# Hybrid mixer layer with grouped experts: weights in 8 KB runs, w2 by rows, combination one step later

## What is computed

```
h   = layer_norm(x) 
mix = hybrid_mixer(h)                # w_in (2048 x 5120), convolutions, gates, w_out (2048 x 2048)
h1  = layer_norm(alpha * h + mix)    # gain ln1_g, shift ln1_b
s   = sigmoid(h1 @ w_router)         # 32 experts in 8 groups of 4
# per token: the best group, and in it the best two experts; gates = s of the two, normalised
ffn = sum over the token's two experts e of gate * ((silu(h1 @ w1[e]) * (h1 @ w3[e])) @ w2[e])
out = layer_norm(alpha * h1 + ffn)   # gain ln2_g, shift ln2_b
```

## Time and profile before

| | |
|---|---|
| median of 3 runs | 1466.75 us (1466.39 to 1469.31) |
| profiled execution, span from first to last instruction | 1466.0 us |
| PE / DVE / ACT / POOL busy | 1296.9 / 455.2 / 353.1 / 243.0 us |
| moved by DMA | 473.81 MB, mean 323 GB/s |
| expert phase, from its first expert product | 419.2 us to about 1448 us |

### The profile page before, as it was taken

How to read it: one execution, slowest core, us unless ns; L and a number is a source line. 1 busy time by engine, 2 the same in 40 slices (tenths; PEclk the granted TensorE clock), 3 DMA queues, 4 the chain that set the end, 5 groups by cost and what they waited for, 6 DMA issues and landing times.

```text
span 1466.0 us, 17030 instructions
## 1 busy us (share of the span) xinstructions
PE 1296.9 (88%) x6870; PEld 721.7 (49%) x6870; DVE 455.2 (31%) x648; ACT 353.1 (24%) x530; POOL 243.0 (17%) x62
## 2 busy tenths in 40 slices
PE   3897989999989999998989898989989898998983
PEld 3887989978743433333433333333433333343331
DVE  5545995642352130311303031121303022130306
ACT  4332322443321121211212121121212121121211
POOL 3767586565100000000000000000000000000001
PEclk9998999999989999999999999999999999999997
DMA  7554535547789999999999999999999999999991
GB/s 275 165 173 144 173 127 189 173 172 251 253 311 387 387 387 387 387 387 387 387 387 387 387 387 387 387 387 387 387 387 387 387 387 387 387 387 387 387 387 76
DMA packets 237572, 473.81 MB, mean 323 GB/s; under 512 B 9594, under 2 KB 10170, under 8 KB 236642
## 3 DMA queue, kind: packets, MB, share of 16 engines
q1 hardware_dynamic: 234256, 471.90, 88.5%
q10 hardware_dynamic: 3282, 1.43, 0.5%
HBM read 471.20 MB, written 2.10 MB: 323 GB/s over the span
## 4 chain that ended last, share of the span: by engine, by line
PE 64%; DMA 13%; DVE 11%; SPq 5%; ACT 4%; issue 2%; POOL 1%; ACTq 0%; DVEq 0%
PE psum L629 16%; PE psum L603 15%; PE psum L643 8%; PE psum L576 8%; PE psum L452 8%; DMA ring<-in_w_dram 7%; PE psum L472 7%; DMA area_g<-in_w_dram 6%; SPq L308 5%; DVE area_g L988 4%; ACT area_c L842 2%; POOL w_low L392 1%; DVE area_a L1252 1%; DVE area_a L1066 1%; DVE area_a L1253 1%
## 5 line engine op out<-in xcount | busy, mean ns | idle before, releaser
L603 PE MATMUL psum<-ring,area_c 128*64 128x512 f32 x1536 | 340.4, 595 | 25.8 <-DMA ring<-in_w_dram 25.8
L392 POOL TENSOR_TENSOR w_low<-ring,w_high 128x2048 fp32r<-128x2048 f32 (+1 forms) x42 | 225.2, 5371 | 112.8 <-ACT w_high L707 112.8
L603 PEld LDWEIGHTS psum<-ring,area_c 128*64 128x64 f32 x1536 | 106.5, 137 | 240.2 <-issue 191.3
L842 ACT ACTIVATE area_c<-psum,ln_chan 128x128 f32<-128x128 f32 x264 | 99.2, 456 | 402.9 <-PE psum L576 402.9
L452 PE MATMUL psum<-in_high,w_high 128*128 128x256 f32 x576 | 168.2, 292 | 25.2 <-POOL w_low L392 9.3
L398 POOL TENSOR_TENSOR area_b<-area_b,area_c 128x1024 f32<-128x1024 f32 x1 | 3.2, 3234 | 1079.1 <-ACT area_b L878 1079.1
L629 PE MATMUL psum<-ring,area_d 128*64 128x512 f32 x768 | 173.3, 596 | 0.4
L452 PE MATMUL psum<-in_low,w_high 128*128 128x256 f32 x576 | 166.8, 290 | 0.0
L452 PE MATMUL psum<-in_high,w_low 128*128 128x256 f32 x576 | 166.7, 289 | 0.0
L643 PE MATMUL psum<-area_d,one_hot_gt 128*128 128x512 f32 x256 | 126.5, 617 | 34.7 <-DVE area_a L1253 23.5
L707 ACT ACTIVATE w_high<-ring 128x2048 fp32r<-128x2048 f32 x56 | 107.0, 1914 | 186.3 <-PE psum L452 114.2
(11 more groups left out here) (178 smaller groups left out, 1055.0 us busy)
## 6 DMA issues: line engine op xcount, KB each, us to landing
ring<-in_w_dram SPq DMA_DIRECT2D x288, 1024.0 KB, 14.4
slot<-in_w_dram SPq DMA_DIRECT2D x48, 1024.0 KB, 14.3
area_g<-in_w_dram SPq DMA_DIRECT2D x48, 1024.0 KB, 14.1
ring<-in_w_in_dram SPq DMA_DIRECT2D x40, 1024.0 KB, 5.1
ring<-in_w_out_dram SPq DMA_DIRECT2D x16, 1024.0 KB, 5.0
area_a<-in_x_dram SPq DMA_DIRECT2D x2, 1024.0 KB, 7.8
out_dram<-area_b SPq DMA_DIRECT2D x4, 512.0 KB, 2.6
area_g<-in_ln_in_g_dram SPq DMA_DIRECT2D x1, 1024.0 KB, 14.9
```

What stands on the lines that cost most here:

```text
L392: nc.gpsimd.tensor_tensor(low[:, tiles], raw_unit(u)[:, tiles], high[:, tiles].bitcast(F32), ALU.subtract).then_inc(pool_low, 1)
L603: mm = pe.matmul(psum[i * CAP:(i + 1) * CAP, j // UNITS, :], gathered[:, kk, i * CAP:(i + 1) * CAP], w[:, i, k, :], start=kk == 0, stop=kk ...
L842: ins = act.activation(gathered[:, k, :], psum[:, 2 + g % 2, k % 4 * P:(k % 4 + 1) * P], ACT.Identity, scale=ln_chan[:, 2, k:k + 1], bias= ...
```

## The change

- **Runs.** A w1 or w3 unit is the same 512 rows, but partition p takes four neighbouring rows (8 KB in one run) in place of rows p, p + 128, p + 256 and p + 384. So that the products match, `gather` reads every fourth channel of a group of 512: its stationary operand has a step of four floats. ACT's gain and shift for the drained channels come in this order from a new tile, `gain`, filled by two DMAs of 16-byte pieces.
- **w2 by rows.** Unit 8 + f is row tile f of w2, whole rows of 8 KB. Its eight products add to all four column blocks, in banks 4 to 7, which complete together in the last unit. `y_sb` has four blocks, copied by `keep_y`.
- **Combination one step later.** The combinations of step `it - 1` follow units 2 to 5 of step `it`, in banks 4 and 5 or 6 and 7 in turn. Those of the last step follow it. DVE's adds move with them. Statistics are taken only in the last step (`done`).
- **ln2's rows** go to `slot0`, loaded when unit 4 of the last step has left it, and no longer before the loop.
- **Written out.** The first 16 steps are written out on SP, PE, ACT and DVE, without a loop; the overflow path keeps a loop of the old kind, with its combinations at once.

```diff
-        y_sb = flat_d[:, 0:2 * CW].rearrange("p (b d) -> p b d", b=2)
-        silu_h, hidden, hidden_2, rt_2 = (flat_d[:, n * CW:(n + 1) * CW] for n in (2, 3, 4, 7))
+        y_sb = flat_d[:, 0:NC * CW].rearrange("p (b d) -> p b d", b=NC)
+        silu_h, hidden, hidden_2, rt_2 = (flat_d[:, n * CW:(n + 1) * CW] for n in (4, 5, 6, 7))
...
-        ln2_scale = area_c[:].rearrange("p k s -> p (k s)")[:, D:2 * D]
-        ln2_shift = [flat_d[:, 5 * CW:7 * CW], sb("ln2_shift1", [P, D // 2])[:]]
-        w_rt, w_scaled = (ln2_shift[1][:, n * KT * E:(n + 1) * KT * E].rearrange("p (k e) -> p k e", k=KT)
+        ln2_scale, ln2_shift = slot0[:, 0:D], slot0[:, D:2 * D]
...
+            for r, src in enumerate((ln1_g[0], ln1_b[0])):
+                sp.dma_start(gain[:, r, :].rearrange("p (q k) -> p q k", q=UNITS),
+                             src.rearrange("(q p k) -> p q k", q=UNITS, p=P)).then_inc(s_gain, 16)
...
-                        src = (w1, w3)[j // 4][0, e].rearrange("(q k p) f -> q p k f", q=4, p=P)[j % 4]
+                        src = (w1, w3)[j // 4][0, e].rearrange("(q p k) f -> q p (k f)", q=4, p=P)[j % 4]
                     else:
-                        src = w2[0, e].rearrange("(f p) (c d) -> c p f d", p=P, c=NC)[j - 8]
-                    sp.dma_start(slot(m)[:, i], src).then_inc(loaded[m % SLOTS], 16)
+                        src = w2[0, e].rearrange("(f p) d -> f p d", p=P)[j - 8]
+                    sp.dma_start(slots[m % SLOTS].rearrange("p (i r) -> p i r", i=2)[:, i], src).then_inc(
+                        loaded[m % SLOTS], 16)
+            def unit_used(it, j):
+                if j < STEP_UNITS - 1:
+                    sp.wait_ge(experts_done, (STEP_UNITS - 1) * it + j + 1)
+                else:
+                    sp.wait_ge(y_ready, NC * it + NC)
...
-            sp.wait_ge(logits_ready, 1)
-            sp.dma_start(ln2_scale, spread(ln2_g[0])).then_inc(s_g2, 16)
-            for h in range(2):
-                sp.dma_start(ln2_shift[h], spread(ln2_b[0][h * D // 2:(h + 1) * D // 2])).then_inc(s_g2, 16)
             sp.wait_ge(x1_ready, 2 * TT)
             load_expert_unit(SLOTS - 1, SLOTS - 1, 0)
-            with sp.Fori(0, PAIRS // TWO - 1) as i2:
-                for n in range(SLOTS, SLOTS + TWO * STEP_UNITS):
-                    sp.wait_ge(experts_done, TWO * STEP_UNITS * i2 + n - SLOTS + 1)
-                    load_expert_unit(n, n % STEP_UNITS, TWO * i2 + n // STEP_UNITS)
-            for m in range((PAIRS - TWO) * STEP_UNITS + SLOTS, PAIRS * STEP_UNITS):
-                sp.wait_ge(experts_done, m - SLOTS + 1)
+            for m in range(SLOTS, PAIRS * STEP_UNITS):
+                unit_used((m - SLOTS) // STEP_UNITS, (m - SLOTS) % STEP_UNITS)
                 load_expert_unit(m, m % STEP_UNITS, m // STEP_UNITS)
+            def load_ln2_rows():
+                for r, src in enumerate((ln2_g[0], ln2_b[0])):
+                    sp.dma_start(slot0[:, r * D:(r + 1) * D], spread(src)).then_inc(s_g2, 16)
...
+                unit_used(PAIRS - 1, STEP_UNITS - SLOTS)
+                load_ln2_rows()
...
-                    k = 4 * g + j
                     for t in range(TT):
                         mm = pe.matmul(psum[:, 2 + g % 2, j * P:(j + 1) * P],
-                                       area_b[:, t, k * P:(k + 1) * P],
+                                       area_b[:, t, g * CW:(g + 1) * CW].rearrange("p (s k) -> p k s", k=UNIT)[:, j, :],
...
+            def combine(it, c):
+                if c < 2:
+                    pe.wait_ge(y_drained, NC * it + 2 * c + 2)
+                    if c == 0:
+                        pe.wait_ge(gt_drained, it + 1)
+                else:
+                    pe.wait_ge(comb_added, NC * it + c - 1)
+                for t in range(TT):
+                    mm = pe.matmul(psum[:, 4 + 2 * (c % 2) + t, :], one_hot_gt[:, t, :], y_sb[:, c, :],
+                                   start=True, stop=True)
+                mm.then_inc(comb_ready, 1)
...
+                    if behind and 2 <= j < 2 + NC:
+                        combine(it - 1, j - 2)
...
+                if behind:
+                    pe.wait_ge(comb_added, NC * it)
+                for f in range(FT):
+                    w = slots[arrived(i2, s, 2 * UNITS + f) % SLOTS].rearrange("p (i c d) -> p i c d", i=2, c=NC)
+                    for c in range(NC):
                         for i in range(2):
-                            mm = pe.matmul(psum[i * CAP:(i + 1) * CAP, 4 + c % 2, :],
-                                           hidden_t[:, f, i * CAP:(i + 1) * CAP], w[:, i, f, :],
+                            mm = pe.matmul(psum[i * CAP:(i + 1) * CAP, 4 + c, :],
+                                           hidden_t[:, f, i * CAP:(i + 1) * CAP], w[:, i, c, :],
                                            start=f == 0, stop=f == FT - 1)
-                            if c == 1 and f == 0 and i == 0:
-                                mm.then_inc(experts_done, 1)
-                    mm.then_inc(y_ready, 1)
-                def combine(c):
-                    pe.wait_ge(y_drained, 4 * it + c + 1)
-                    if c == 0:
-                        pe.wait_ge(gt_drained, it + 1)
-                    else:
-                        pe.wait_ge(comb_added, 4 * it + c)
-                    for t in range(TT):
-                        mm = pe.matmul(psum[:, 6 + t, :], one_hot_gt[:, t, :], y_sb[:, c % 2, :],
-                                       start=True, stop=True)
-                        if t == 0 and c != NC - 2:
-                            mm.then_inc(experts_done, 1)
-                    mm.then_inc(comb_ready, 1)
-                project(0)
-                project(1)
-                combine(0)
-                project(2)
-                combine(1)
-                combine(2)
-                project(3)
-                combine(3)
+                        if f == FT - 1:
+                            mm.then_inc(y_ready, 1)
+                    if f < FT - 1:
+                        mm.then_inc(experts_done, 1)
...
+            for it in range(PAIRS):
+                step(it // TWO, it % TWO, it > 0, it < PAIRS - 1)
+            for c in range(NC):
+                combine(PAIRS - 1, c)
...
-                                             ACT.Identity, scale=ln_chan[:, 2, k:k + 1], bias=ln_chan[:, 3, k:k + 1])
+                                             ACT.Identity, scale=gain[:, 0, k:k + 1], bias=gain[:, 1, k:k + 1])
...
+            def keep_y(it):
+                for c in range(NC):
+                    act.wait_ge(y_ready, NC * it + c + 1)
+                    act.activation(y_sb[:, c, :], psum[:, 4 + c, :], ACT.Copy).then_inc(y_drained, 1)
...
+            def add_combined(it, done):
                 for c in range(NC):
...
+                    at = 4 + 2 * (c % 2)
+                    v.tensor_tensor(area_a[:, 0, cols], area_a[:, 0, cols], psum[:, at, :], ALU.add)
+                    v.tensor_tensor(area_a[:, 1, cols], area_a[:, 1, cols], psum[:, at + 1, :],
                                     ALU.add).then_inc(comb_added, 1)
+                    if done:
+                        dve.wait_ge(comb_added, NC * it + c + 1)
+                        v.bn_stats(stats[:, 0, c, :], area_a[:, 0, cols])
+                        v.bn_stats(stats[:, 1, c, :], area_a[:, 1, cols]).then_inc(stats_done, 1)
...
+            for it in range(PAIRS):
+                gate_slots(it, it > 0)
+                if it < PAIRS - 1:
+                    place_ahead(it)
+                if it > 0:
+                    add_combined(it - 1, False)
+                hide(it)
```

More of the change, by code:

```diff
@@ L166, in hybrid_layer @@
         ln_chan = sb("ln_chan", [P, 4, KT])
+        gain = sb("gain", [P, 2, KT])
         ident = sb("ident", [P, P])
@@ L395, in _ @@
             pool.wait_ge(normed, 2 * TT * 2 + 1)
-            pool.wait_ge(s_g2, 16 * 3)
+            pool.wait_ge(s_g2, 16 * 2)
             last = area_b[:, TT - 1, D // 2:]
@@ L399, in _ @@
             pool.wait_ge(y_out_scaled, 1)
-            nc.gpsimd.tensor_tensor(last, last, ln2_shift[1], ALU.add).then_inc(y_out_pool, 1)
+            nc.gpsimd.tensor_tensor(last, last, ln2_shift[:, D // 2:], ALU.add).then_inc(y_out_pool, 1)
         CONSTS = 10
@@ L580, in gather, with arrived, step @@
                 mm.then_inc(gather_ready, 1)
-            def step(i2, s):
-                it = TWO * i2 + s
[L585 to L590, removed]
+            def arrived(i2, s, j):
+                n = STEP_UNITS * s + j
+                fills = TWO * STEP_UNITS // SLOTS
+                pe.wait_ge(loaded[n % SLOTS], 32 * fills * i2 + 32 * (n // SLOTS + 1))
+                return n
+            def combine(it, c):
[9 more added lines that the diff above has]
+                mm.then_inc(comb_ready, 1)
+            def step(i2, s, behind, ahead):
+                it = TWO * i2 + s
                 for j in range(2 * UNITS):
+                    if j < UNITS:
```

(89 more changed lines are left out.)

25 lines of the change are left out of this document (10 added, 15 removed).

## The result

The changed kernel takes 1524.24 us (median of 4, 1521.41 to 1526.42) against 1467.33: ratio 1.0382, 95% interval 1.0366 to 1.0398. I had forecast 1397; the slower rival, strided weight loads, is what happened, 27 us beyond its 1497.

What follows compares the result with a forecast made beforehand. Expert transfers bound, TensorE 3.4 us a step behind: 428.0 start + 932.7 for 388.0 MB at 416 GB/s + 1.1 + 0.5 + tail 16.0 + 18.15 = 1396.4 span, 1397 us time; range 1383 to 1440.

Steps and rivals of the forecast that it cites:

- the slower rival: Gathers' strided weight loads on TensorE decide: 1,024 loads at 105 ns, 107 us, time 1497 us; chance 0.19.
- Part 5: Gathers' stationary operand read every fourth float: taken to cost 0; other end 113 ns more per 128-column load.
- Rival A: TensorE's strided gather weight loads cost 107 us on top of span 1388.6, time 1497 us; chance in full 0.19.
- Part 1: Expert transfers in 8 KB runs: 416 GB/s (408 to 422) instead of 387, step 65.0 to 60.5 us.
- Part 2: TensorE's step in the expert phase: waits for DVE's adds and ACT's copy go, period 61.6 to 59.5 us.
- The transfers bound, narrowly: Expert phase after the change: transfers' step of 60.5 us stays 1.0 above TensorE's 59.5.
- rival B: Expert transfers exceed 421 GB/s, so TensorE bounds the kernel: 1389 us; chance 0.17.
- Part 4: Tail after the last unit: last projection to end of statistics grows from 8.9 to 16.0 us; 18.15 us after stays.
- Part 3: Other edits (statistics, LayerNorm 2 rows, written-out loop) at nothing, except 0.45 MB more instruction fetch, 1.1 us of transfer.

Runs made afterwards that it cites:

- the mended kernel: The changed kernel with ACT writing the normalised rows in gather order once, so gathers read contiguous floats, and DVE's scaled residual reading that order: 1395.51 us, ratio 0.9504.
- step eight: The changed kernel with gathers reading every eighth float, 32 bytes apart (channels no longer match, only time counts): one run, 1525.98 us.

## Why the prediction was wrong

- **The step that failed** is Part 5: "I take 0, since PE reads through its own path". The bound beside it was right: DVE's row said 0.9 ns an element, and PE paid (67.59 - 59.80) / 64 = 122 ns a load, 0.95 ns a column. I had shown myself that 128 columns fill the gathers' spacing, so that nothing could hide it, and then gave that end 0.19 on the strength of a path that no row showed. That sentence was an assertion where the nearest row spoke the other way.
- **Rival A's size.** It had 1388.6 + 107. The span is 1519.7, 131 above 1388.6. The first mark stands 5.5 us later (454.50 against 449.03): 4.4 is the stride, since without it the mark stands at 450.15, and 1.1 is not; the contiguous gather has it too, because TensorE's clock rose later than in the kernel before and its first 48 loads took 8.53 us against 7.07. Fifteen steps average 67.92 against 59.5, that is 15 x 7.8 for the stride, 15 x 0.3 for PE's own step, and some 5 for the clock; the tail from the last mark is 0.7 shorter. 5.5 + 126.3 - 0.7 = 131. The stride alone is 4.4 + 117 = 121 against the rival's 107, which took 105 ns a load, after 8 ns that "might hide"; it paid 122, and nothing hid.
- **Part 1** right in kind, small in size: 421 GB/s for 8 KB runs, where I took 416 with 422 as the end. An 8 KB packet takes 8192 x 16 / 421 = 311 ns, so 9.2 ns go with each packet saved, not 8.
- **Part 2** right: both waits gone, 59.80 measured in the contiguous gather against 59.5. The 0.3 that it missed: the units of w1 and w3 take 28.4 us of the chain with the combinations between them, against 27.8 in one piece before, and shorter pieces elsewhere give about half of that back.
- **"The transfers bound, narrowly"**: with the stride away they tie, 59.8 and 59.8. The forecast of 1397 for the mechanism I believed is 1.5 us from what the mended kernel takes, 1395.5; it was the forecast of another kernel. Even there the nearness is partly luck: with 421 for 416 my sum of transfers gives 1386, and the chain of the mended kernel is TensorE's, for which rival B had 1389.
- **Part 4**: the last projection's last unit to the end of the statistics took 16.0 us by my count, 15.7 in the trace of the changed kernel (lines below). **Part 3**: instruction packets 25 to 56, 0.51 MB more against 0.45; no gaps. The two loads of `gain` took 5.0 us each.

```profile
1485.79 3.60 PE L659 MATMUL psum<-area_g,area_d 128*64 128x512 f32 x16
...
1500.79 0.68 DVE L1295 BATCH_NORM_STATS2 stats<-area_a 128x6 f32<-128x512 f32 x1
```

## What to carry to other kernels

A layout that makes a transfer's run longer moves the stride somewhere else. Look which engine reads it, how often, and whether that read already fills its slot: here a gain of 5 us a step in the queue was paid for with 7.8 us on the engine that stood 3.4 us behind it. Read fp32 at most every second float (every fourth cost TensorE, ACT and DVE alike, and every second was tried on weight loads alone), and where an order must be changed, change it once, in an instruction that already writes the data and has slack. And where the only row for an unseen operation names a price, take that price until a row says otherwise.

## What the runs showed of the hardware

- A strided fp32 read at 16 bytes costs about 0.8 to 0.95 ns an element more on all three engines seen: weight loads 122 ns for 128 columns, the moving stream 0.91 ns a column, ACT 0.94 ns an element, DVE 0.8 to 0.9. At 8 bytes a weight load pays 6 ns, at 32 bytes 6 ns more than at 16.
- The strided weight load takes the same time at both levels of TensorE's clock, the contiguous one does not. The first 48 loads of the expert phase begin at granted clock 0.50. Strided, they took 11.44 us, 238 ns each, though the clock was at 0.50 for more than half of that time; at full clock it is 7.68 / 32 = 240. Contiguous, they took 8.53 us; the clock was at 0.50 until 418, and if those after it ran at the 118 ns of full clock, the others took some 220 ns each, an estimate from this trace. So at 0.50 the stride costs some 20 ns a load and at 1.00 it costs 122. Each pair of rows has the loads in the chain and the window in which the clock rises or has not yet risen, first for the changed kernel, then for the contiguous gather:

```profile
411.37 11.44 PE psum L589 x48
417.00:418.00 1.00, 1.00 (x7) 1.00 (x6) 0.98 (x1) 0.05 (x1) 0.00 (x0) 0.62 0.00 0
...
411.88 8.53 PE psum L589 x48
417.00:418.00 1.00, 1.00 (x7) 1.00 (x7) 0.96 (x2) 0.23 (x1) 0.00 (x0) 0.50 0.00 0
```

- TensorE's clock falls to half for between three and four us in three of the changed kernel's steps, each 1.6 us longer. In one, the windows show it full until 1004, at 0.50 from 1005 to 1008, full from 1009:

```profile
1004.00:1005.00 1.00, 0.42 (x4) 0.23 (x4) 0.00 (x0) 0.92 (x3) 0.00 (x0) 0.93 0.06 25
1005.00:1008.00 3.00, 3.00 (x8) 0.97 (x10) 0.43 (x1) 0.38 (x1) 0.00 (x0) 0.50 0.01 5
1008.00:1009.00 1.00, 1.00 (x6) 0.28 (x4) 0.00 (x0) 0.00 (x0) 0.00 (x0) 0.87 0.00 0
```

  Ahead of it stand 7.7 us of slow gathers, four transposes and 1.25 us of waiting, but they stand so in every step. It is the clock's lower level, 1.2 GHz. Between 430 and 1340 us the kernels with contiguous or step-two gathers have no such fall, nor has the one with strided combinations; the changed kernel, step eight and the kernel before with the stride have two, two and five (the changed kernel's third and a sixth of the kernel before with the stride come later). Why some steps and not others was not tried.
